# Placing one-hot batches partly on ScalarE, and moving dot products out of the tail of the output projection

## The reference

```
h = RMSNorm(x) * (1 + scale) + shift;  [q k v x_rg y_rg] = h @ w_in
x = x + gate_mix * (concat(attention, rglru) @ w_out)            # output projection
h = RMSNorm(x) * (1 + scale_ffn) + shift_ffn
# PEER feed-forward: 8 heads, product keys 128 x 128 = 16384 experts, 16 chosen per head
s = h @ w_q, against sub_keys;  top 16 of each half;  top 16 of the 256 sums -> expert (key1, key2), softmax weight
x = x + gate_ffn * sum over the 128 chosen experts e of  g_e * gelu(h . u[e]) * v[e]
y = RMSNorm(x)
```

## Time and profile before

| | us |
|---|---|
| median of 3 runs | 3731.07 |
| lowest and highest of them | 3713.43, 3742.76 |
| the profiled execution | 3692.98 |
| its span in the trace | 3690.8 |
| output projection of the latent tokens, in the span | about 895 to 1066 |
| routing of the latent tokens | about 1066 to 1516 |
| placing | about 1516 to 1740 |
| experts and final norm | about 1740 to 3690 |

### The profile page before, as it was taken

How to read it: one execution, slowest core, us unless ns; L and a number is a source line. 1 busy time by engine, 2 the same in 40 slices (tenths; PEclk the granted TensorE clock), 3 DMA queues, 4 the chain that set the end, 5 groups by cost and what they waited for, 6 DMA issues and landing times. The chain is left out here.

```text
span 3690.8 us, 47451 instructions
## 1 busy us (share of the span) xinstructions
PE 3145.2 (85%) x15281; PEld 2078.6 (56%) x15281; DVE 2639.8 (72%) x5949; ACT 1050.1 (28%) x1821; POOL 1982.2 (54%) x1776
## 2 busy tenths in 40 slices
PE   6875999698969898476578899998999999999994
PEld 4654445465433333366356666666767666766663
DVE  2328687796556878999677787877878787876446
ACT  4631244464110011366112222222222222222112
POOL 0002555354238885221477677776777677775542
PEclk9887999899989999688789999999999999999997
DMA  9341876677659994286999999999999999999996
GB/s 332 136 138 65 280 254 230 200 229 243 243 206 332 326 318 174 97 248 199 372 372 369 371 408 408 404 388 397 408 398 408 378 406 399 408 407 378 364 344 239
DMA packets 408631, 1133.01 MB, mean 307 GB/s; under 512 B 34040, under 2 KB 125432, under 8 KB 408368
## 3 DMA queue, kind: packets, MB, share of 16 engines
q0 software_dynamic: 221184, 805.40, 58.7%
q1 hardware_dynamic: 171424, 317.82, 23.7%
q10 hardware_dynamic: 15888, 8.13, 0.7%
HBM read 1077.51 MB, written 53.71 MB: 306 GB/s over the span
## 5 line engine op out<-in xcount | busy, mean ns | idle before, releaser
L2317 POOL DMA_INDIRECT exp_value_row<-in_v_rows,exp_v_id x568 | 710.5, 1251 | 277.9 <-issue 175.1
L2364 DVE CUSTOM_DVE_ANT_0 edge_row<-edge_row,edge_x 128x1024 f32<-128x1024 f32 x480 | 584.0, 1218 | 300.1 <-DMA edge_row<-in_u_rows,edge_u_id 266.2
L2309 POOL DMA_INDIRECT edge_row<-in_u_rows,edge_u_id x480 | 516.8, 1077 | 325.1 <-DVE edge_dot L2364 173.9
L379 POOL DMA_INDIRECT ahead_row<-in_u_rows,keep_expert_id x256 | 327.0, 1277 | 359.0 <-DVE keep_dot L389 296.9
L2198 PE MATMUL exp_a_ps<-exp_xT_hi,exp_u_hi 128*128 128x512 f32 x1024 | 409.9, 400 | 19.0 <-DVE exp_u_lo L2333 9.9
L2213 PE MATMUL exp_o_ps<-exp_v_hi,exp_w_hi 128*128 128x512 f32 x1024 | 337.8, 412 | 85.2 <-DVE keep_acc L2428 85.2
L2198 PE MATMUL exp_a_ps<-exp_xT_lo,exp_u_hi 128*128 128x512 f32 x1024 | 401.3, 392 | 0.0
L2198 PE MATMUL exp_a_ps<-exp_xT_hi,exp_u_lo 128*128 128x512 f32 x1024 | 401.1, 392 | 0.0
L2428 DVE TENSOR_TENSOR keep_acc<-exp_o_ps,keep_acc 128x1024 f32<-128x1024 f32 x256 | 311.5, 1220 | 109.0 <-PE exp_o_ps L2213 107.5
L389 DVE CUSTOM_DVE_ANT_0 ahead_row<-ahead_row,ahead_x 128x1024 f32<-128x1024 f32 x256 | 304.7, 1221 | 74.2 <-DMA ahead_row<-in_u_rows,keep_expert_id 70.5
L2184 PE MATMUL exp_v_ps<-exp_value_row,exp_hot 128*32 128x512 f32 x2272 | 279.3, 603 | 59.9 <-DMA exp_value_row<-in_v_rows,exp_v_id 59.7
(11 more groups left out here) (385 smaller groups left out, 5152.9 us busy)
## 6 DMA issues: line engine op xcount, KB each, us to landing
edge_u_raw<-in_uT SPq DMA_DIRECT2D x130, 512.0 KB, 7.0
exp_v_raw<-in_v_rows SPq DMA_DIRECT2D x128, 512.0 KB, 6.6
exp_g_raw<-scratch_g SPq DMA_DIRECT2D x128, 256.0 KB, 8.3
scratch_g<-place_grid SPq DMA_DIRECT2D x3, 8192.0 KB, 36.1
proj_ctx_mod_slab<-in_w_mod SPq DMA_DIRECT2D x8, 2048.0 KB, 15.4
heads_early_room<-in_w_in SPq DMA_DIRECT2D x10, 1024.0 KB, 10.9
exp_value_row<-in_v_rows,exp_v_id POOLq DMA_INDIRECT x568, 7.7
mod_slab<-in_w_mod SPq DMA_DIRECT2D x4, 2048.0 KB, 20.3
```

What stands on the lines that cost most here:

```text
L379: nc.gpsimd.indirect_dma_start(out=ahead.row[:, n % KEY_RING, :], out_offset=None, in_=io["u_rows"], in_offset=bass.IndirectOffsetOnAxis(a ...
L2309: nc.gpsimd.indirect_dma_start(out=key_row[:, j % RING, :], out_offset=None, in_=io["u_rows"], in_offset=bass.IndirectOffsetOnAxis(ap=u_id ...
L2317: nc.gpsimd.indirect_dma_start(out=value_row[:, 4 * (j % 2) + t, :], out_offset=None, in_=io["v_rows"].rearrange("a b n -> (a b) n"), in_o ...
L2364: nc.vector.tensor_tensor_reduce(out=key_row[:, j % RING, :], in0=key_row[:, j % RING, :], in1=x, scale=1.0, scalar=0.0, op0=ALU.mult, op1 ...
```

## The change

In the output projection the 48 dots stay and keep their order, but 15 instead of 8 come ahead of the gates' wait, the first three pairs have 5 + 3 + 3 instead of 4 + 3 + 3, and the last pair has none. In placing, in every second step batch 2's scaled side is made by ACT: it computes (iota - key)^2 into the buffer and then Relu(weight - weight * square), which is the weight where the square is 0 and nothing where it is 1 or more. DVE only makes the plain side of that batch. The negated keys and weights that ACT needs are made once by four small DVE instructions. In all steps ACT now copies batches 2 and 3 of the step before between the two scalings, and batches 0 and 1 after them.

```diff
@@ out_projection, DVE @@
-            dots(8)
+            dots(15)
             dve.wait_ge(gate_ready, GATES)
...
-                dots(4)
                 if i + 1 < PAIRS:
+                    dots(5)
                     residual(c, i + 1)
                 for j in range(2):
-                    dots(3)
+                    if i + 1 < PAIRS:
+                        dots(3)
                     dve.wait_ge(turned, 2 * i + j + 1)
@@ place_weights @@
-    SCALED_BY_ACT, SCALED_BY_DVE = (0, 2), (1, 3)
+    SCALED_BY_ACT, SCALED_BY_DVE, SOMETIMES_BY_ACT = (0, 2), (1, 3), 2
...
+        minus = s.sb("minus", [P, DENSE_TILES, 2, STEPS * BATCH])
...
+        def made_by_act(before, b):
+            return b == SOMETIMES_BY_ACT and before % 2 == 1
@@ DVE @@
+            for t in range(DENSE_TILES):
+                mine_by_act = cols[:, t, 0:3:2, :].rearrange("p n (m s) -> p n m s", s=STEP)\
+                    [:, :, :, SOMETIMES_BY_ACT * BATCH:(SOMETIMES_BY_ACT + 1) * BATCH]
+                last = nc.vector.tensor_scalar(minus[:, t, :, :].rearrange("p n (m s) -> p n m s", s=BATCH),
+                                               mine_by_act, -1.0, None, ALU.mult)
+            last.then_inc(minus_ready, 1)
...
-                    if b in SCALED_BY_ACT:
+                    if made_by_act(before, b):
+                        nc.vector.tensor_tensor(
+                            hot[:, b, 1, :, :], keep["iota"][:, :].unsqueeze(1).broadcast_to([P, BATCH, N_KEYS]),
+                            cols[:, t, 1, at:at + BATCH].unsqueeze(2).broadcast_to([P, BATCH, N_KEYS]), ALU.is_equal)\
+                          .then_inc(hot_ready, 1)
+                    elif b in SCALED_BY_ACT:
@@ PE @@
                         pe.wait_ge(scaled, 2 * before + SCALED_BY_ACT.index(b) + 1)
+                        if made_by_act(before, b):
+                            pe.wait_ge(hot_ready, 2 * before + SCALED_BY_ACT.index(b) + 1)
@@ ACT @@
+            def make_batch(t, m, before, b):
+                act.wait_ge(made, BATCHES * (before - 1) + b + 1)
+                for k in range(BATCH):
+                    last = nc.scalar.activation(hot[:, b, 0, k, :], keep["iota"][:, :], ACT.Square,
+                                                bias=minus[:, t, 0, m * BATCH + k:m * BATCH + k + 1])
+                last.then_inc(squared, 1)
+                act.wait_ge(squared, before // 2 + 1)
+                for k in range(BATCH):
+                    at = m * STEP + b * BATCH + k
+                    last = nc.scalar.activation(hot[:, b, 0, k, :], hot[:, b, 0, k, :], ACT.Relu,
+                                                scale=minus[:, t, 1, m * BATCH + k:m * BATCH + k + 1],
+                                                bias=cols[:, t, 2, at:at + 1])
+                last.then_inc(scaled, 1)
...
+            def body(t, m, before):
+                scale_batch(t, m, before, 0)
+                if before:
+                    copy_batches(before - 1, (2, 3))
+                make_batch(t, m, before, 2) if made_by_act(before, 2) else scale_batch(t, m, before, 2)
+                if m == 0 and t >= 2:
+                    act.wait_ge(stored[t % 2], 16 * (t // 2))
+                copy_batches(before, (0, 1))
             walk(body)
+            copy_batches(TOTAL - 1, (2, 3))
```

More of the change, by code:

```diff
@@ L1856, in place_weights @@
         made = s.sem("made")
+        squared = s.sem("squared")
+        minus_ready = s.sem("minus_ready")
         placed = s.sem("placed")
@@ L1936, in _ @@
             act.wait_ge(cols_ready, DENSE_TILES)
-            def body(t, m, before):
-                if m == 0 and t >= 2:
-                    act.wait_ge(stored[t % 2], 16 * (t // 2))
-                for b in SCALED_BY_ACT:
-                    at = m * STEP + b * BATCH
-                    act.wait_ge(hot_ready, 2 * before + SCALED_BY_ACT.index(b) + 1)
-                    for k in range(BATCH):
-                        last = nc.scalar.activation(hot[:, b, 0, k, :], hot[:, b, 0, k, :], ACT.Copy,
-                                                    scale=cols[:, t, 2, at + k:at + k + 1])
-                    last.then_inc(scaled, 1)
-                for b in range(BATCHES):
-                    act.wait_ge(made, BATCHES * before + b + 1)
+            act.wait_ge(minus_ready, 1)
@@ new lines, in scale_batch @@
+            def scale_batch(t, m, before, b):
+                at = m * STEP + b * BATCH
+                act.wait_ge(hot_ready, 2 * before + SCALED_BY_ACT.index(b) + 1)
+                for k in range(BATCH):
+                    last = nc.scalar.activation(hot[:, b, 0, k, :], hot[:, b, 0, k, :], ACT.Copy,
+                                                scale=cols[:, t, 2, at + k:at + k + 1])
+                last.then_inc(scaled, 1)
[6 more added lines that the diff above has]
+                act.wait_ge(squared, before // 2 + 1)
+                for k in range(BATCH):
+                    at = m * STEP + b * BATCH + k
+                    last = nc.scalar.activation(hot[:, b, 0, k, :], hot[:, b, 0, k, :], ACT.Relu,
+                                                scale=minus[:, t, 1, m * BATCH + k:m * BATCH + k + 1],
+                                                bias=cols[:, t, 2, at:at + 1])
+                last.then_inc(scaled, 1)
@@ L1950, in body, with copy_batches @@
+            def copy_batches(step, batches):
+                t, m = step // STEPS, step % STEPS
+                for b in batches:
+                    act.wait_ge(made, BATCHES * step + b + 1)
                     nc.scalar.activation(grid[t % 2][:, :, m * STEP + b * BATCH:m * STEP + (b + 1) * BATCH],
```

## The result

The changed kernel took 3701.8 us (median of 13 runs, 3691.9 to 3720.6) against 3731.8 us (13 runs of the kernel before in the same comparison). The ratio is 0.9933, with a 95% interval of 0.9915 to 0.9951, so 18 to 32 us less. The prediction had -21.6 us, a median of 3709.5 in a range of 3684 to 3734, and the same verdict. A second comparison on another chip, where the kernel before takes 3692.7, gave 0.9912 (0.9897 to 0.9928), so 27 to 38 us less; -21.6 lies outside that interval.

The account below looks back on a forecast made before the run. It took DVE to bound the output projection's tail, and a PE-ACT chain slightly longer than DVE's loop to bound placing. Terms -11.5 - 8.6 - 2.1 + 0.6 = -21.6 us; 3731.1 - 21.6 = 3709.5 us, range 3684 to 3734.

Parts of the forecast that it names:

- The tail: End of the output projection: without ten dots, DVE waits for half the transposes, then runs two modulations; -11.5 us.
- Seven dots moved forward: Output projection, ahead of the gates' wait: tile 0's residual comes later, but with six us of cover; 0.
- Fifth dots: Output projection, pairs 0, 1, 2: one more dot each may wait for its gather, with 4 us of cover; 0.
- DVE's shorter comparison: Placing: in 16 of 32 steps a 1024 wide comparison becomes 512 wide, -0.54 us each; -8.6 us.
- ACT's order: Placing: scaling batch 0 no longer stands behind the last two copies, so the 1.85 us chain is gone; -2.1 us.
- The last step: Placing's last step: 9.6 us before, the last copy now ending at 9 to 9.8 us; 0.
- The prediction's lower-clock case: Placing's last step: at the lower clock PE finishes batches 2 and 3 at 9.2 us, instead of 8.2.
- Four small instructions: Ahead of placing's loop: four small DVE instructions cost between 0 and 2.4 us, put at +0.6.
- Rival (a): Placing: PE becomes the bound, at worst 229 us, +10; total -1, 3730 us; 7 in 100.
- Rival (b): Only one half works, output projection or placing; -10 or -11.5, 3720 us; 8 in 100.
- Rival (c): Placing: ACT chains it, 253 us, +34; total +23, 3754 us, slower than before; 3 in 100.
- The estimate of 0.41 us for each small ACTIVATE: Placing: by the skill page's price ACT takes 13.9 us for two steps, placing 222 us; total -7.5; 3 in 100.

Follow-up runs that it names:

- front_24: Changed kernel with 24 instead of 15 dots ahead of the wait for the gates; ratio 0.9957 to the kernel before.
- make_only: Kernel before with ACT making batch 2 in every second step of placing, copies in the old order, dots unmoved; ratio 1.0005 to the kernel before.
- order_only: Kernel before with only ACT's copies moved in placing, every batch 2 scaled as before, dots unmoved; ratio 0.9977 to the kernel before.
- after_again: The changed kernel once more, unchanged, on a second chip; ratio 0.9912 to the kernel before.
- tail_only: Kernel before with only the dots of the output projection moved, placing unchanged; ratio 0.9958 to the kernel before.
- place_only: Changed kernel with the dots of the output projection put back, so only placing is changed; ratio 0.9961 to the kernel before.
- every_step: Changed kernel with ACT making batch 2 in every step but the first, instead of every second; ratio 0.9901 to the kernel before.

## Why the prediction was right

- **The tail** (-11.5): measured -11.2 from first instruction to routing (170.6 to 159.4), and 158.4 to 160.1 in all kernels with it except front_24, 167.6 to 172.8 in those without. The step "DVE waits for the first half of the transposes, then two modulations" is what the rows show, to 0.2 us.
- **Seven dots moved forward, nothing**: right, but the cover was 3.8 us, not 6. The seven moved dots came 2.48 us apart and not 2.13. Why is open: the DMA engines were as full in one stretch as in the other (busy share 1.04 and 1.03). front_24 shows what stood behind it.
- **Fifth dots, nothing**: right for the sum, with less to spare than said. Their gathers waited up to 4.51 us, not 2.7. They ate 2.9 of 5.93 us ahead of tile 5's residual and all 5.65 ahead of tile 7's, which came 0.4 us late.
- **DVE's shorter comparison** (-8.6): steps of 6.14 and 6.67 us, as said. make_only shows that it counts only together with ACT's order. The first step is 7.13 us, and that and a few of 6.86 keep the 31 steps at 199.8, about 1 us above the terms.
- **ACT's order** (-2.1): order_only has 206.8 for 208.9 us in the 31 steps, -2.1; with its shorter last step placing is 3.3 us shorter. The claim that two loops of nearly one length ran side by side was the part of the prediction most open to doubt, and order_only with make_only shows it.
- **The last step** (0): measured +1.2, but -0.5 in after_again. In the first profile ACT had made batch 2 by 6.3 us into the step, as predicted, and PE then took 3.78 us for two batches, at a granted clock of 0.52. The prediction's lower-clock case, PE through at 9.2, was too short by its own price: two batches at 1.78 us are 3.6, so 9.9. PE was through at 10.2, and at 8.5 in after_again. The price of Relu, put at the scaling's, is no part of this: its 0.09 us more each is in both.
- **Four small instructions** (+0.6): the loop starts 0.4 later.
- **Sum**: placing -7.5 in the first profile, -9.5 in the second, -10.2 in the pair that ends after it; predicted -10.1. Output projection and placing together -19 to -21, predicted -21.6. The first interval of the timed ratio, 18 to 32 us, holds that, and the second, 27 to 38, doesn't.
- **What the prediction did not have**: the timed medians moved by 30 us on two chips. The pair without experts puts the surplus behind placing, where the prediction had nothing, and where no profile shows it; its cause is open. That the measured median lies within the predicted range is owed to the width that the scatter of the runs had given it.

Rival (a), PE as the bound, fails: DVE waits for PE nowhere in the loop, and the granted clock rose. Rival (b), only one half works, fails by tail_only and place_only. Rival (c), ACT as the bound, fails too, and every_step shows by how much: ACT had room for 15 more makings. Four scalings in a row take 1.28 us, though each lasts 0.39, since the next starts before the last has ended. The estimate of 0.41 us for each small ACTIVATE, by the Trainium skill (ScalarE: Activation LUTs, Rules for kernel authors), fits how long one with one pointer lasts here (390 to 393 ns), and not what a row of them costs.

## What to carry to other kernels

Before cutting work on the engine that looks full, follow the loop through the other engines: here a chain of PE, copy and scaling had nearly the same period, and the two edits were worth 3 us and nothing alone, and 8 to 10 together. An in-order engine's last copies of a step should not stand in front of the first work of the next step when another engine waits for that. Work that only fills gaps belongs where its engine waits for others, and not behind the last thing the stage needs; how much fits in front is set by the first consumer, and can be estimated from the trace. Look at the whole path to the last instruction: here six dots stayed on it.

## What the runs showed of the hardware

- A second pointer operand (scale and bias) costs an ACTIVATE of 128 x 128 about 0.09 us: 482 against 390 ns, four in 1.65 against 1.28 us.
- Gathers of 128 rows of 4 KB into a ring of four gave a dot every 2.13 us for the first eight and every 2.48 for the next seven, while weight loads ran, and still left 4.51 us of waiting for a fifth in a row later on.
- Two batches of placing's last step, 16 matmul records, took PE 3.78 us at a granted clock of 0.52 in one execution and 2.05 at full clock in another. That is most of the 2 us between their placing stages.
- The kernel before took 3732 us in the first comparison and 3691 to 3694 in the later ones, on three chips. The changed kernel's experts stage was 1947 us at 374 GB/s in the first and 1911 at 381 in after_again. So totals of profiles from two occasions say nothing on a change. Whether it was the chip is not shown.
